# Sample attention of a two-layer decoder step: whole pages in one transfer, turned keys stored in place, two queues sharing each quarter of the cache

## The reference

```python
past_c = cache_cmp[page_table].reshape(Bd, PAST_LEN, 2, KV_HEADS, HEAD_DIM)
...
o_c = einsum('bgrqn,bngd->bqgrd', masked_softmax(q . kc_blk), vc_blk)      # compressed branch
imp_s = ...                                   # importance of each block of 64 tokens
_, idx = lax.top_k(score, 16)                 # 16 of 33 blocks
s_s = einsum('bqgrd,bgqnkd->bgrqnk', q, kv_g[..., 0, :]) * scale            # selected branch
o_s = einsum('bgrqnk,bgqnkd->bqgrd', p_s, kv_g[..., 1, :])
kw = concatenate([win_state, kvw], axis=1)                                  # 512 + 8 tokens
o_w = einsum('bgrqk,bkgd->bqgrd', p_w, kvw[:, :, 1])                        # window branch
return gates0 * o_c + gates1 * o_s + gates2 * o_w
```

## Time before and how its profile is read

| | |
|---|---|
| three runs | 1146.55, 1150.43, 1152.43 us; median 1150.43 |
| profiled execution | 1158.34 us, span 1156.7 us |
| PE busy (matmul) | 1025.1 us, 89% of the span |
| VectorE / ScalarE / GpSimd busy | 603.5 / 297.5 / 109.8 us |
| moved by the DMA engines | 147.78 MB in the whole span |
| sample attention | 891 to 1085 us of the span |

### The profile page before, as it was taken

One profiled execution on the slowest core, in us unless ns is written; L12 is line 12 of the kernel. 1 busy time (PEld: TensorE's weight loads), 2 busy tenths in 40 slices (PEclk: granted clock), 3 DMA queues, 4 the chain that ended last, 5 costly groups with the idle time before them and its releaser, 6 DMA issues.

```text
span 1156.7 us, 18963 instructions
## 1 busy us (share of the span) xinstructions
PE 1025.1 (89%) x6558; PEld 632.2 (55%) x6558; DVE 603.5 (52%) x1341; ACT 297.5 (26%) x721; POOL 109.8 (9%) x197
## 2 busy tenths in 40 slices
PE   4999999999879979899999987768988698898897
PEld 2476676776544444675574474435545455565443
DVE  2205889776445655896000025268885456555213
ACT  4210001010430131111101124246663334433102
POOL 0000000000000000000000023200000444432000
PEclk9999999999879989999999978779999899999899
DMA  7443664353514565763012111420001878866202
GB/s 313 142 113 110 182 182 126 105 165 114 184 46 101 163 243 190 205 181 110 5 69 73 37 55 38 143 73 1 1 1 46 254 235 261 248 203 206 103 1 82
DMA packets 55964, 147.78 MB, mean 128 GB/s; under 512 B 10441, under 2 KB 38602, under 8 KB 49098
## 3 DMA queue, kind: packets, MB, share of 16 engines
q1 hardware_dynamic: 49738, 129.89, 35.5%
q0 software_dynamic: 6144, 16.79, 4.6%
HBM read 139.63 MB, written 15.27 MB: 134 GB/s over the span
## 4 chain that ended last, share of the span: by engine, by line
PE 62%; DVE 16%; DMA 6%; SPq 6%; issue 6%; ACT 4%; POOL 0%; DVEq 0%; ACTq 0%; POOLq 0%
PE PS L1131 55%; PE PS L1134 7%; DMA arena<-in_ccmp 3%; SPq L648 3%; SPq L649 2%; DVE arena L1725 2%; DVE arena L1726 2%; DVE arena L2002 2%; DVE arena L1983 2%; ACT arena L1045 1%; DVE arena L1696 1%; DMA arena<-in_win 1%; DMA arena<-in_cmem 1%; DVE arena L1728 1%; DVE arena L1815 1%
## 5 line engine op out<-in xcount | busy, mean ns | idle before, releaser
L1131 PE MATMUL PS<-arena 128*32 128x64 f32 (+16 forms) x5460 | 862.2, 383 | 38.8 <-DVE arena L1736 6.7
L1131 PEld LDWEIGHTS PS<-arena 128*128 128x128 f32 (+5 forms) x5460 | 499.2, 153 | 384.5 <-issue 243.3
L1134 PE MATMUL PS<-arena 128*128 128x128 f32 (+3 forms) x1098 | 178.5, 307 | 85.2 <-ACT arena L810 15.2
L1134 PEld LDWEIGHTS PS<-arena 128*128 128x128 f32 (+3 forms) x1098 | 134.1, 156 | 132.0 <-issue 82.2
L1725 DVE TENSOR_TENSOR arena<-arena 128x2048 f32<-128x2048 f32 x32 | 73.2, 2288 | 19.9 <-DMA arena<-in_ccmp 18.8
L779 POOL DMA_DIRECT2D arena<-in_csel x128 | 68.8, 538 | 99.4 <-issue 99.4
L1726 DVE TENSOR_TENSOR arena<-arena 128x2048 f32<-128x2048 f32 x32 | 73.1, 2285 | 0.0
L1913 DVE SCALAR_TENSOR_TENSOR arena<-arena 128x576 f32<-128x576 f32 x8 | 5.8, 756 | 129.0 <-ACT arena L964 128.8
L1045 ACT ACTIVATE arena<-arena 128x512 f32<-128x512 f32 (+3 forms) x96 | 52.7, 552 | 36.8 <-DVE arena L1983 36.6
L1983 DVE CUSTOM_DVE_ANT_0 arena<-PS,arena 128x512 f32<-128x512 f32 (+3 forms) x96 | 41.2, 486 | 6.3 <-PE PS L1131 6.3
L1881 DVE TENSOR_TENSOR arena<-arena,PS 128x512 f32<-128x512 f32 x16 | 11.0, 687 | 63.9 <-PE PS L1131 63.8
(11 more groups left out here) (180 smaller groups left out, 563.1 us busy)
## 6 DMA issues: line engine op xcount, KB each, us to landing
arena<-in_wall SPq DMA_DIRECT2D x20, 2048.0 KB, 9.6
arena<-in_ccmp SPq DMA_DIRECT2D x128, 256.0 KB, 3.8
arena<-in_csel SPq DMA_DIRECT2D x128, 128.0 KB, 3.0
arena<-in_csel POOLq DMA_DIRECT2D x128, 128.0 KB, 3.3
arena<-in_cmem SPq DMA_DIRECT2D x32, 256.0 KB, 3.9
arena<-in_win SPq DMA_DIRECT2D x8, 1024.0 KB, 6.4
out_win_s<-in_win SPq DMA_DIRECT2D x1, 8064.0 KB
arena<-in_xp SPq DMA_DIRECT2D x1, 2048.0 KB, 16.5
```

The costliest lines, as they stand in the source:

```text
L1131: return nc.tensor.matmul(out, lhsT, rhs, start=start, stop=stop, skip_group_check=True)
L1134: return nc.tensor.transpose(out, in_, ident[0:in_.shape[0], 0:in_.shape[0]])
```

## The change

A page's keys and values are loaded together in one transfer of 128 rows of 2 KB into one of 2 x 4 quarter buffers `SKV[t % 2][c]` (4 pages each). The turned keys of a quarter are written back over its keys (`SKV[..][.., 0:256]`); the values stay beside them. `SK`, `SV`, `SKT` and `SQB` go, and with `SQB` POOL's copy of the queries: PE reads `QZ` itself. The SP queue loads pages 0 and 1 of every quarter and POOL pages 2 and 3, each with a semaphore of its own for each quarter (`sa_lo`, `sa_hi`); PE waits for both at every second key tile. Quarter c of turn t may be loaded when group c + 2 of back(t-2) is done. Groups of the back are put in another order: compressed, window 0, new, window 1; then quarters 0 to 3; then new, window 2, window 3. VectorE therefore adds the window's part to `SO` behind the last group. There are three window buffers. Turn 0's pages and window are all issued before `pa_mix` 6 (its quarter 2 once the probabilities of the 10th of 12 units are turned, its quarter 3 once those of the 11th are, its window behind the last scores). SP's and POOL's loops are written out, with constant page addresses. The load of the second block of output weights waits for group 2 of the last back, no longer for its end.

```diff
+        SKV = [[at(o, 2048).rearrange("p (s c) -> p s c", s=4) for o in quads]
+               for quads in ((8192, 10240, 0, 2048), (4096, 12288, 14336, 16384))]
...
+        def quad_load(eng, t, c, pages, loaded):
+            if t >= 2:
+                eng.wait_ge(sa_used, START.sa_used + 6 * (t - 2) + c + 2)
+            for s in pages:
+                page = eng.value_load(ptab[0:1, NPG * t + 4 * c + s:NPG * t + 4 * c + s + 1], min_val=0, max_val=POOL - 1)
+                eng.dma_start(SKV[t % 2][c][:, s, :], I["csel"][bass.ds(page, 1), :, :].rearrange("a p c -> (a p) c")
+                              ).then_inc(loaded[t % 2][c], 16)
...
-            keys(Turn(0, 0, 2))
+            quad_load(sp, 0, 0, range(2), sa_lo)
+            quad_load(sp, 0, 1, range(2), sa_lo)
+            sp.wait_ge(pa_t, BANKS_OF_P * (UNITS - 2))
+            quad_load(sp, 0, 2, range(2), sa_lo)
+            sp.wait_ge(pa_t, BANKS_OF_P * (UNITS - 1))
+            quad_load(sp, 0, 3, range(2), sa_lo)
+            sp.wait_ge(pa_s, PT * UNITS)
+            window(0)
             sp.wait_ge(pa_mix, 6)
-            window(Turn(0, 0, 2))
-            window(Turn(0, 1, 2))
-            keys(Turn(0, 1, 2))
-            with sp.Fori(1, NB // 2) as i:
-                for n in range(2):
-                    keys(Turn(i, n, 2))
-                    window(Turn(i, n, 2))
+            for t in range(1, NB):
+                for c in range(4):
+                    quad_load(sp, t, c, range(2), sa_lo)
+                window(t)
...
-            for n in range(2):
-                sp.wait_ge(sa_used, START.sa_used + 6 * (NB - 1 + n))
-                load_w(B_OUT1 + n)
+            sp.wait_ge(sa_used, START.sa_used + 6 * (NB - 1))
+            load_w(B_OUT1)
+            sp.wait_ge(sa_used, START.sa_used + 6 * (NB - 1) + 2)
+            load_w(B_OUT1 + 1)
...
+            for t in range(1, NB):
+                for c in range(4):
+                    quad_load(pool, t, c, range(2, 4), sa_hi)
...
-                            nc.scalar.copy(SKT[:, :, 256 * j:256 * j + 256],
-                                           PS[:, 6 + j % 2, :].rearrange("p (g c) -> p g c", g=2)).then_inc(sa_fa, 1)
+                            nc.scalar.copy(SKV[t.n % 2][j // 2][:, 2 * (j % 2):2 * (j % 2) + 2, 0:256],
+                                           PS[:, 6 + j % 2, :].rearrange("p (q c) -> p q c", q=2)).then_inc(sa_fa, 1)
...
-                        if j % 4 == 0:
-                            pe.wait_ge(sa_k[j // 4], t.value(128, 128))
+                        if j % 2 == 0:
+                            pe.wait_ge(sa_lo[n][j // 2], 32 * (t.i + t.n // 2 + 1))
+                            pe.wait_ge(sa_hi[n][j // 2], 32 * (t.i + t.n // 2 + 1))
...
-                    return [(c, 0, 512, SKT[:, :, 512 * c:512 * c + 512])]
+                    return [(c, 0, 512, lambda p, gp: SKV[t.n % 2][c][p:p + 64, :, 128 * gp:128 * gp + 128])]
...
-                tiles += [(SM[:, 128 * j:128 * j + 128], SV[n][:, j, :], sel, j == 0, j == NPG - 1) for j in range(NPG)]
-                tiles.insert(7, (SM[:, 2048:2112], Vn[0:NS, 0, :], sel, False, False))
+                late = tiles[4:]
+                tiles[4:] = [(SM[:, 128 * j:128 * j + 128], SKV[n][j // 4][:, j % 4, 256:512], sel, j == 0, False)
+                             for j in range(NPG)]
+                tiles += [(SM[:, 2048:2112], Vn[0:NS, 0, :], sel, False, True)] + late
...
-                dve.wait_ge(sa_used, t.value(6, 2, base=START.sa_used))
+                dve.wait_ge(sa_used, t.value(6, 1, base=START.sa_used))
                 dve.wait_ge(sa_y, t.value(1, 0, base=START.sa_y))
                 lk.link(ts(SO, PS[:, 1, 0:HD], rs(170, 171), None, ALU.mult))
-                lk.link(stt(SO, PS[:, 1, HD:2 * HD], rs(159, 160), SO, ALU.mult, ALU.add))
                 took(5)
                 dve.wait_ge(sa_used, t.value(6, 6, base=START.sa_used))
+                lk.link(stt(SO, PS[:, 1, HD:2 * HD], rs(159, 160), SO, ALU.mult, ALU.add))
                 stt(SO, PS[:, 0, 0:HD], rs(158, 159), SO, ALU.mult, ALU.add).then_inc(sa_mix, 1)
```

More of the change, by code:

```diff
@@ L306, in build @@
         KCp = at(25728, 128).rearrange("p (g n) -> p g n", g=2)
[L308 to L321, removed]
+        SKV = [[at(o, 2048).rearrange("p (s c) -> p s c", s=4) for o in quads]
+               for quads in ((8192, 10240, 0, 2048), (4096, 12288, 14336, 16384))]
+        SWKT = at(18432, 1024).rearrange("p (g c) -> p g c", g=2)
+        SM = at(19456, 2112)
+        SIMP = at(21568, 130)
+        SCH = at(21698, 128)
+        SSC = at(21826, 40)
+        SMB = at(21866, 40)
+        SM8 = at(21906, 8)
+        SNM = at(21914, 64)
+        SS2 = at(21978, 40)
+        SO = at(22018, HD)
+        SPC = [at(31808, 128), at(22082, 128)]
+        SWI = [at(o, 2048).rearrange("p (s c) -> p s c", s=4) for o in (26112, 28160, 6144)]
         SPT = [at(30208 + 512 * n, 512).rearrange("p (s c) -> p s c", s=4) for n in range(2)]
         SW = at(31232, 576)
-        SPC = [at(31808, 128), at(20756, 128)]
-        SO = at(20500, HD)
         gfin = at(8192, 1024)
@@ L643, in _ @@
             sp.wait_ge(kv_stored, KV_STORED)
[L644 to L650, removed]
-            def window(t):
-                sp.wait_ge(sa_used, t.value(6, -6, base=START.sa_used))
-                sp.dma_start(SWI[t.n], I["win"][bass.ds(t.at(1), 1)].rearrange("a (s p) c -> (a p) s c", p=128)
-                             ).then_inc(sa_w[t.n], 16)
-            keys(Turn(0, 0, 2))
-            sp.wait_ge(pa_mix, 6)
-            window(Turn(0, 0, 2))
-            window(Turn(0, 1, 2))
-            keys(Turn(0, 1, 2))
-            with sp.Fori(1, NB // 2) as i:
-                for n in range(2):
-                    keys(Turn(i, n, 2))
-                    window(Turn(i, n, 2))
-            for n in range(2):
-                sp.wait_ge(sa_used, START.sa_used + 6 * (NB - 1 + n))
-                load_w(B_OUT1 + n)
+            def window(t):
+                if t >= 3:
+                    sp.wait_ge(sa_used, START.sa_used + 6 * (t - 2))
+                sp.dma_start(SWI[t % 3], I["win"][t:t + 1].rearrange("a (s p) c -> (a p) s c", p=128)
+                             ).then_inc(sa_w[t % 3], 16)
+            quad_load(sp, 0, 0, range(2), sa_lo)
[6 more added lines that the diff above has]
+            window(0)
+            sp.wait_ge(pa_mix, 6)
+            for t in range(1, NB):
[6 more added lines that the diff above has]
+            load_w(B_OUT1 + 1)
             sp.wait_ge(sz_done, 1)
@@ L761, in _ @@
             nc.gpsimd.memset(HT[:, 2:8, SEQ + NS:TOK], 0.0).then_inc(ht_zero, 1)
[L763 to L766, removed]
-            pool.wait_ge(pa_mix, 6)
[L769 to L780, removed]
+            pool.wait_ge(cp_phi, NB + 1)
+            pool.wait_ge(r_turned, 12)
+            quad_load(pool, 0, 0, range(2, 4), sa_hi)
+            quad_load(pool, 0, 1, range(2, 4), sa_hi)
+            pool.wait_ge(pa_t, BANKS_OF_P * (UNITS - 2))
+            quad_load(pool, 0, 2, range(2, 4), sa_hi)
+            pool.wait_ge(pa_t, BANKS_OF_P * (UNITS - 1))
+            quad_load(pool, 0, 3, range(2, 4), sa_hi)
+            pool.wait_ge(pa_mix, 6)
+            for t in range(1, NB):
+                for c in range(4):
+                    quad_load(pool, t, c, range(2, 4), sa_hi)
         @block.scalar
@@ L1567, in front @@
             def front(t, prev):
-                n = t.n % 2
+                n, number = t.n % 2, t.at(1)
                 pe.wait_ge(sa_ba, t.value(3, -3, base=START.sa_ba))
@@ L1603, in middle @@
             def middle(t):
-                n = t.n % 2
+                number = t.at(1)
                 pe.wait_ge(sa_fa, front_value(t, 9, "A"))
@@ L1624, in part, with new @@
                 def part(c):
-                    return [(c, 0, 512, SKT[:, :, 512 * c:512 * c + 512])]
-                both([(4, 0, 512, SWKT)], [(5, 128 + 64 * s, 64, Kn[:, s]) for s in range(2)]).then_inc(sa_part, 1)
-                if 2 * t.i + n:
+                    return [(c, 0, 512, lambda p, gp: SKV[t.n % 2][c][p:p + 64, :, 128 * gp:128 * gp + 128])]
+                def new(s):
+                    return 5, 128 + 64 * s, 64, lambda p, gp: Kn[p:p + 64, s, gp, :]
+                both([(4, 0, 512, lambda p, gp: SWKT[p:p + 64, gp, :])], [new(0), new(1)]).then_inc(sa_part, 1)
+                if number:
                     out_turn(t.value(1, 0))
```

37 lines of the change are left out of this document (17 added, 20 removed).

## The result

The changed kernel is 0.5% slower: 1158.80 us against 1153.42 us, medians of 19 runs each, ratio 1.0050 with a 95% interval of 1.0033 to 1.0068. A second series on another occasion gave 1.0034 (1.0009 to 1.0059). The prediction was 1136.0 us, from a median of 1150.43 us over three runs of before; over 19 runs that median is 3.0 us higher.

What follows compares the result with a forecast made beforehand. The prediction took SP's slow issue of page transfers, which PE waits for, as the bound. 21.5 - 0.3 - 0.8 - 6.0 = 14.4 us less gave 1150.43 - 14.4 = 1136.0 us, with an 8-in-10 range of 1128 to 1146.

Steps and rivals of the forecast that it cites:

- What bounds the kernel before: Sample attention stage, 891 to 1085 us: PE waits for SP's slow issue; at most 21.5 us saved.
- undisturbed turn: Sample attention on PE: a turn without a transfer wait lasts 20.46 us, the base for the savings.
- What it adds on PE: PE's path: 0.3 us for the last turn's window addition, 0.8 us for more waits; the split score read taken as free.
- the 0.8 us for waits: PE's path: five more wait instructions a turn, taken at 0.1 us a turn, 0.8 us in all.
- Rival 4: Score matmuls on PE: the broken-up read slows them and uses up the gain; 1145 to 1159 us, chance 0.05.
- Early work: Loads for turns 0 and 1: turn 0's pages issued during the prompt's attention, turn 1's in time; no stall taken.
- SP and POOL: Issue queues: 1.07 us an issue on SP, 1.24 on POOL; both in time, POOL with 1.3 us to spare.
- Rival 3: POOL's queue: issue time grows with the bytes, to 2.48 us a page; 24 us slower, 1174, chance 0.05.
- Do the pages come in time?: Page and window transfers against the next front: 1.0 us late in each of six fronts, 6.0 us in all.
- rival 2: Page transfers stay the bound at 350 GB/s: 15.6 us of stalls, only 4.8 us less, 1145.6 us; chance 0.18.
- The sum in the stage: Sample attention stage: 21.5 - 0.3 - 0.8 - 6.0 = 14.4 us less.
- figure of about 358 GB/s: Memory-side rate for a turn's 5.24 MB: 14.6 us, 2.2 us of stall a turn, median near 1143; not used in the sum.

Runs made afterwards that it cites:

- the kernels without waits: Two edits of the changed kernel: keys loaded before values with each window a turn ahead (1143.26 us, again 1141.21), and keys only (1132.55 us).
- keys only: Changed kernel with the next window issued after key tile 7, and the values of turns 2 to 7 left out: 1132.55 us, ratio 0.9828.
- the version with keys first: Changed kernel with all keys of a turn issued before its values and each window one turn ahead: 1143.26 us, ratio 0.9923; again 1141.21 us.

## Why the prediction was wrong

Point by point, by its own steps:

- *What bounds the kernel before*: right. SP's issue and the window were last in its stage, and the undisturbed turn of 20.46 us is PE's floor; it is 20.3 us in the kernels without waits. The end product of that step, 21.5 us to be saved "if every page is there in time", holds for a typical run with 17 to 20 us (190.1 - 173.2, 190.1 - 170.6). It was 2.0 to 4.6 us too large, since the profile of before had a slow stage (193.8 us, where the second has 190.1); 0.3 of it is the addition in the last turn, which the sum charged elsewhere.
- *What it adds on PE*: right, and small. The undisturbed turn is 0.16 us shorter than before, so the 0.8 us for waits didn't appear. The 0.3 us in the last turn did: PE waits 0.73 us for VectorE before its last transpose, 0.41 before. Rival 4 falls: the 320 score matmuls of 64x512 take 594 ns a piece after and 593 before, with the read in four runs.
- *Early work*: right but for one wait. Turn 0 cost 13.55 us and nothing was late for it; turn 1's pages were in time, its window 0.44 us late.
- *SP and POOL*: right. 1.07 us forecast for SP, 1.0 to 1.1 measured (8.02 us for eight); POOL's step is 1.15 us for whole pages, 1.24 forecast. Rival 3 falls.
- *Do the pages come in time?* This is the step that failed. It put the lateness at 1.0 us a turn, 6.0 us in all; it is 3.8 us (24.1 less 20.3), which makes 18 to 20 us from front(1) to front(7). With the stalls of front(7) itself the stage takes 20.5 to 23.2 us more than in the kernels without waits (193.8 less 173.2 or 170.6), and that eats up the whole gain. Three terms of it were off. First the rate: 390 GB/s is what the full engines reach, but over the burst it is 345, near the 350 GB/s that the prediction kept for rival 2. That alone makes the last byte 1.7 us later. (The working of the 390 has a slip: (158 - 46.8) / 3 is 37.1 ns for each KB, not 36.2; 2 KB rows then take 84 ns, which is the 390 GB/s used.) Second the landing: I allowed 1.9 us from the earlier trace rows behind an idle engine, and priced only the last byte against the window. But a page waits in the crowd for 6 us, so quarters 2 and 3 are late as well, and they come before the window in the same front. Third the assumption that stalls of a microsecond leave the clock alone: in front(2) it is at the 1.2 GHz level for some 3 us behind the second of them. The price can be estimated from PE's busy time in the stage: 161.5 and 159.1 us in the two profiles of the changed kernel, 156.3 with keys only, so 3 to 5 us of the loss are slower work and the rest is waiting.
- *Rival 2* had the right bound, the transfers, and gave 1145.6 us; the measured time is 13 us beyond it, and outside the range. It charged 2.6 us a turn, where 3.8 are lost, and took 20.4 us as the gain without stalls, where a typical run has 17 to 20.
- The range missed because none of its cases, rivals included, weighed one thing. The kernel before loads values a whole turn ahead of their use, and keys as soon as the turn before has turned its own. The change binds both to the release by the back two turns earlier, some 10 us before the front needs them (by the prediction's own figures 988.79 to 998.41 for quarter 0, 992.2 to 1002.4 for quarter 3), where it knew that 5.24 MB take 13.4 us. The prediction weighed only the end of that interval. The runs with the release moved, with half the bytes and with keys first show that this is the cause: not the late release alone, since the version with keys first has the same release and no waits to speak of, but the values that must land with the keys in that time.
- *The sum in the stage*: forecast 14.4 us less, measured 3.7 us more (second profiles), 18.1 us apart. Stalls of 20.5 to 23.2 us instead of 6.0 account for 14.6 to 17.2 of them, the gain taken too large for the other 4.3 to 1.7, and the 0.8 us for PE's waits goes the other way. The 3.0 us by which the first median lay low are separate.
- The Trainium skill's figure of about 358 GB/s for the memory side ("DMA: Bandwidth & Descriptors", section "Where 436 GB/s comes from") would have given 1143. The trace holds 393 GB/s for two microseconds and 345 over the burst, so its size was fair for the mean and not a cap.

What stays open: how the slower first microseconds of the burst divide between the release in four steps and the queues' start, and whether the slow clock would go with shorter stalls alone. Neither was tried by itself.

## What to carry to other kernels

Before merging two transfers, ask when each half is needed and when its place comes free: the merged one is issued at the later of the two releases and is due at the earlier of the two needs. Compare the bytes with that interval, not with the whole turn; a stage whose DMA engines are idle a third of the time, as here, can still be bound by transfers. And where the need comes in pieces, price the landing of each piece in the crowd, not only the last byte.

## What the hardware showed that was not expected

- A page of 256 KB took from 2.5 us (the shortest) over 5.4 us (the median) to 8.2 us (the longest) from issue to landing, over the 128 transfers of the changed kernel, while the rate in the windows of the burst stayed under 400 GB/s.
- In the second profile of the version with keys first and the window ahead, one turn took 26.02 us instead of 20.3. PE stopped for 2.3 us in the middle of a group, with nothing in the profile to wait for, and the granted clock behind it was 0.50 for more than 6 us:

```profile
976.57 0.31 PE L1142 MATMUL PS<-arena 128*32 128x64 f32 x7
979.22 0.55 PE L1142 MATMUL PS<-arena 128*32 128x64 f32 x25 [2.34 <-issue]
...
980.15 5.14 PE L1142 MATMUL PS<-arena 128*32 128x64 f32 x80
...
985.57 4.84 PE L1142 MATMUL PS<-arena 64*32 64x512 f32 x32
...
982.00:988.00 6.00, 6.00 (x35) 1.34 (x31) 1.90 (x14) 0.00 (x0) 2.75 (x6) 0.50 0.81 241
```

In an undisturbed turn the rows at 980.15 and 985.57 take 3.28 and 3.64 us. One short stop cost 5.7 us, more than half of it as slower work. Stops of this kind, 0.94, 1.06, 1.30 and 2.34 us long, stand two in each profile of this version and lengthen four of its turns; in the turns from front(1) to front(7) of the other profiles there is none of that length. Why PE stopped isn't shown.
